# Streaming encoder step on one core: sums by pairs in three LayerNorms, high halves first, and a store for each output tile

## The reference, cut to what matters

```python
h = layernorm(x, ln_in_g, ln_in_b)
p = h @ w_in                                  # RWKV-7 columns, then q, k, v, f of FoX attention
mix = concat(rwkv7(p_r), fox(p_f)) @ w_out
h = layernorm(alpha * h + mix, ln1_g, ln1_b)
q = h @ peer_w_q                              # 8 heads; scores, top 16 of 16384 experts per head
act = gelu(peer_u[idx] . h)
h = layernorm(alpha * h + sum(gate * act * peer_v[idx]), ln2_g, ln2_b)
```

## Time and profile before

| | |
|---|---|
| median of 3 runs | 1433.5 us (1433.44 to 1434.15) |
| the profiled execution's own time | 1433.6 us |
| its span in the profile | 1431.9 us |
| PE busy | 1381.3 us, 96% of the span |
| DVE, ACT, POOL busy | 987.8, 685.0, 494.0 us |
| mean granted clock of PE | 0.994 of 2.4 GHz |

### The profile page before, as it was taken

One profiled execution on the slowest core, in us unless ns is written; L12 is line 12 of the kernel. 1 busy time (PEld: TensorE's weight loads), 2 busy tenths in 40 slices (PEclk: granted clock), 3 DMA queues, 4 the chain that ended last, 5 costly groups with the idle time before them and its releaser, 6 DMA issues.

```text
span 1431.9 us, 34642 instructions
## 1 busy us (share of the span) xinstructions
PE 1381.3 (96%) x11341; PEld 1320.5 (92%) x11341; DVE 987.8 (69%) x2303; ACT 685.0 (48%) x1455; POOL 494.0 (34%) x664
## 2 busy tenths in 40 slices
PE   7999999889999999999999999999999999999996
PEld 5977787778899999999999999999999999999995
DVE  5348776675699995888888888856555555555555
ACT  4665533223436666544444444444444544444444
POOL 4000021111538998766666666652000000000000
PEclk9999999999999999999999999999999999999999
DMA  4352110004324445444444444445555555555552
GB/s 137 125 144 81 60 46 3 3 10 163 102 76 118 140 139 144 136 124 118 120 122 117 120 122 118 123 133 147 148 152 147 148 151 147 149 152 147 148 152 81
DMA packets 85224, 168.69 MB, mean 118 GB/s; under 512 B 9850, under 2 KB 11402, under 8 KB 84970
## 3 DMA queue, kind: packets, MB, share of 16 engines
q1 hardware_dynamic: 85162, 167.84, 40.6%
HBM read 164.80 MB, written 2.97 MB: 117 GB/s over the span
## 4 chain that ended last, share of the span: by engine, by line
PE 55%; POOL 23%; issue 12%; DVE 6%; ACT 2%; POOLq 1%; DMA 0%; ACTq 0%; SPq 0%; DVEq 0%
POOL hlo L635 23%; PE PS L1040 15%; PE PS L1042 15%; PE PS L1041 15%; PE PS L1134 1%; PE PS L1035 1%; POOLq L633 1%; PE PS L1028 1%; DVE TT L1533 1%; PE PS L1299 1%; PE PS L1422 1%; DVE FSQ L1733 1%; DVE GSD L1696 1%; PE PS L1316 1%; PE PS L1314 0%
## 5 line engine op out<-in xcount | busy, mean ns | idle before, releaser
L635 POOL TENSOR_TENSOR hlo<-hraw,hhiq 128x256 fp32r<-128x256 f32 x512 | 397.2, 785 | 145.1 <-ACT hhiq L678 143.2
L1040 PE MATMUL PS<-H1h,hhiq 128*128 128x320 f32 x1024 | 343.6, 336 | 3.9 <-POOL hlo L635 3.4
L678 ACT ACTIVATE hhiq<-hraw 128x256 fp32r<-128x256 f32 x508 | 211.4, 418 | 257.1 <-PE PS L1042 228.4
L1042 PE MATMUL PS<-H1h,hlo 128*128 128x320 f32 x1024 | 315.4, 308 | 0.0
L1041 PE MATMUL PS<-H1l,hhiq 128*128 128x320 f32 x1024 | 315.1, 308 | 0.0
L1042 PE MATMUL PS<-Wh,hlo 128*128 128x320 f32 x1016 | 314.0, 309 | 0.0
L1040 PEld LDWEIGHTS PS<-H1h,hhiq 128*128 128x128 f32 x1024 | 193.6, 189 | 9.2 <-POOL hlo L635 7.0
L1041 PEld LDWEIGHTS PS<-H1l,hhiq 128*128 128x128 f32 x1024 | 193.4, 189 | 0.0
L1042 PEld LDWEIGHTS PS<-H1h,hlo 128*128 128x128 f32 x1024 | 192.2, 188 | 0.0
L1042 PEld LDWEIGHTS PS<-Wh,hlo 128*128 128x128 f32 x1016 | 190.7, 188 | 0.0
L1953 DVE TENSOR_SCALAR oh<-iotak,pair 128x128 f32<-128x128 f32 x320 | 128.6, 402 | 48.4 <-PE PS L1458 43.8
(11 more groups left out here) (324 smaller groups left out, 2543.9 us busy)
## 6 DMA issues: line engine op xcount, KB each, us to landing
hraw<-in_uT SPq DMA_DIRECT2D x256, 256.0 KB, 2.6
hraw<-in_vE SPq DMA_DIRECT2D x254, 256.0 KB, 2.6
wraw<-in_wbig SPq DMA_DIRECT2D x50, 512.0 KB, 3.8
xin<-in_xT SPq DMA_DIRECT2D x4, 336.0 KB, 4.3
out_yT<-XF SPq DMA_DIRECT2D x4, 320.0 KB
ckx<-in_ckT SPq DMA_DIRECT2D x2, 512.0 KB, 7.6
vs<-in_cv SPq DMA_DIRECT2D x1, 768.0 KB, 8.5
out_ko<-kx SPq DMA_DIRECT2D x1, 672.0 KB
```

Source lines behind the costliest of these rows:

```text
L635: nc.gpsimd.tensor_tensor(hlo[q // 2 % 4][:, cols_], hraw[q // 2 % 4][:, cols_], hhiq[q % 4][:].bitcast(F32), ALU.subtract).then_inc(s_hlo ...
L678: return nc.scalar.activation(out, in_, f, **kw)
L1040: mm(out, whi_, xhi, start=start, stop=False)
L1042: return mm(out, wlo_, xhi, start=False, stop=stop)
```

## The change

It has six parts.

1. **Sums by pairs.** In norm 0 DVE adds x in pairs as its parts land and PE sums two tiles instead of eight. In every norm the squares of tiles 4 and 5, and of 6 and 7, are added on DVE (`norm_pairs`) so that PE sums six tiles instead of eight. In norm 2 POOL adds tiles 0 to 3 of XF (XS4) and DVE tiles 6 and 7 (XS2), and PE sums four.
2. **Ones in front.** PE begins with `hold(7, 8)`.
3. **Order of the loads.** x goes before `colv`; the first weights before the small matrices, which get a semaphore of their own (`s_rest`). POOL makes the low half of item 0.
4. **High half first.** The V products and those of items 34 and 35 do the two matmuls with the high half of an activation tile when that is there, and the one with the low half after it. In w_q's case the high halves of the weights 35 and 36 are made ahead of the squares, and 37 behind them.
5. **The last sums.** DVE makes XF tile by tile as each bank is finished (`s_fin`). ACT loads the table for the root beforehand. DVE applies gain and bias to tiles 6 and 7.
6. **Stores.** One store for each of the 8 tiles.

```diff
-NORM_ORDER = [list(range(KT)), list(range(KT)), [2, 3, 0, 1, 4, 5, 6, 7]]
+PAIRS = ((0, 1, 2, 3, 4, 6), (0, 1, 2, 3, 4, 6), (0, 1, 2, 3, 4, 6))
-POOL_ITEMS = [*range(I_WQ, N_ITEMS)]
+POOL_ITEMS = [0, *range(I_WQ, N_ITEMS)]
...
+                if i == 0:
+                    sp.dma_start(wfs[:], wf).then_inc(s_small, 16)
...
-            for q in range(4):
-                sp.wait_ge(s_yf, 2 * q + 2)
-                sp.dma_start(yT[:, 2 * q:2 * q + 2, N_META:T], XF[:, 2 * q:2 * q + 2, :]).then_inc(s_out, 16)
+            for j in (0, 1, 2, 3, 4, 6, 5, 7):
+                if j < KT - 2:
+                    sp.wait_ge(s_yf, j + 1)
+                else:
+                    sp.wait_ge(s_yd, j - KT + 3)
+                sp.dma_start(yT[:, j, N_META:T], XF[:, j, :]).then_inc(s_out, 16)
...
+            for k in range(1, 4):
+                pool.wait_ge(s_xf, k + 1)
+                if k > 1:
+                    pool.wait_ge(s_xs4, k - 1)
+                nc.gpsimd.tensor_tensor(XS4[:], XF[:, 0, :] if k == 1 else XS4[:], XF[:, k, :], ALU.add).then_inc(s_xs4, 1)
...
-            for i in range(I_WO + 2, I_WQ + 1):
+            for i in range(I_WO + 2, I_WQ + 3):
                 whi_of(i)
             norm_squares(1, X1, SQ1)
-            whi_of(I_WQ + 1)
+            whi_of(I_WQ + 3)
...
             pe.wait_ge(s_onesg, 1)
-            for j in range(KT):
-                pe.wait_ge(s_x[j // (KT // XQ)], 16)
-                mean_part(0, j, xin, ones)
+            hold(7, 8)
+            for q in range(0, XQ, 2):
+                pe.wait_ge(s_xp, q // 2 + 1)
+                ins = mm(PS[:, MEAN_BANK, 0:T], ones[:], SQ0[:, q, :], start=(q == 0), stop=(q == XQ - 2))
+            ins.then_inc(s_mean, 1)
...
+            for q in range(XQ):
+                dve.wait_ge(s_x[q], 16)
+                pair = tt(SQ0[:, q, :], xin[:, 2 * q, :], xin[:, 2 * q + 1, :], ALU.add)
+                if q % 2:
+                    own(pair)
+                    tt(SQ0[:, q - 1, :], SQ0[:, q - 1, :], SQ0[:, q, :], ALU.add).then_inc(s_xp, 1)
+            norm_center(0, xin)
+            norm_pairs(0, SQ0)
...
+            def norm_pairs(n, S):
+                for k in (4, 6):
+                    dve.wait_ge(s_sq, KT * n + k + 2)
+                    tt(S[:, k, :], S[:, k, :], S[:, k + 1, :], ALU.add).then_inc(s_sqp, 1)
...
+            mean = PS[:, MEAN_BANK, 0:TQ]
+            for j in (4, 5):
                 pe.wait_ge(s_xf, j + 1)
-                mean_part(2, j, XF, ones2)
+                mm(mean, ones2[:], XF[:, j, :], start=(j == 4), stop=False)
+            pe.wait_ge(s_xs4, 3)
+            mm(mean, ones2[:], XS4[:], start=False, stop=False)
+            pe.wait_ge(s_xs2, 1)
+            mm(mean, ones2[:], XS2[:], start=False, stop=True).then_inc(s_mean, 1)
```

More of the change, by code:

```diff
@@ L273, in build @@
         SDF = last.put("SDF", [P, TQ])
+        XS4 = last.put("XS4", [P, TQ])
+        XS2 = last.put("XS2", [P, TQ])
         m = Region(BASE, TAIL)
@@ L680, in norm_squares @@
             def norm_squares(n, X, S):
-                for j, k in enumerate(NORM_ORDER[n]):
+                for j, k in enumerate(range(KT)):
                     act.wait_ge(s_xc, KT * n + j + 1)
@@ L1014, in _ @@
                     down(k * 2 + e, e, k * 16 + 16 * e)
+            act.wait_ge(s_onesg, 2)
+            act.wait_ge(s_down, NI)
+            own(A(SDF[:, 0:1], ones2[:, 0:1], ACT.Sqrt))
             norm_squares(2, XF, SQF)
             norm_root(2, SDF[:])
-            for j in range(KT):
+            for j in range(KT - 2):
                 act.wait_ge(s_nr, 2 * KT + j + 1)
@@ L1026, in mean_part @@
             def mean_part(n, j, X, c1):
-                ins = mm(PS[:, MEAN_BANK, 0:X.shape[2]], c1[:], X[:, NORM_ORDER[n][j], :], start=(j == 0), stop=(j == KT - 1))
+                ins = mm(PS[:, MEAN_BANK, 0:X.shape[2]], c1[:], X[:, j, :], start=(j == 0), stop=(j == KT - 1))
                 if j == KT - 1:
@@ L1032, in variance @@
             def variance(n, S, c1):
-                for j, k in enumerate(NORM_ORDER[n]):
-                    pe.wait_ge(s_sq, KT * n + j + 1)
-                    ins = mm(PS[:, VAR_BANK, 0:S.shape[2]], c1[:], S[:, k, :], start=(j == 0), stop=(j == KT - 1))
+                for k in PAIRS[n]:
+                    if k < 4 or len(PAIRS[n]) == KT:
+                        pe.wait_ge(s_sq, KT * n + k + 1)
+                    else:
+                        pe.wait_ge(s_sqp, 2 * sum(len(x) < KT for x in PAIRS[:n]) + k // 2 - 1)
+                    ins = mm(PS[:, VAR_BANK, 0:S.shape[2]], c1[:], S[:, k, :], start=(k == 0), stop=(k == PAIRS[n][-1]))
                 ins.then_inc(s_var, 1)
@@ L1153, in _ @@
                     k = 2 * i + kk
+                    w, v = whi[hi_slot(i)][:, 512 * kk:512 * kk + 512], wlo[raw_slot(i)][:, 512 * kk:512 * kk + 512]
+                    pe.wait_ge(s_hhi, k + 1)
+                    for b, t0 in enumerate(V0):
+                        mm(PS[:, 4 + b, :], hTh[:, k, t0:t0 + P], w, start=(k == 0), stop=False)
+                        mm(PS[:, 4 + b, :], hTh[:, k, t0:t0 + P], v, start=False, stop=False)
                     pe.wait_ge(s_hlo, k + 1)
                     for b, t0 in enumerate(V0):
[L1156 to L1158 removed]
+                        ins = mm(PS[:, 4 + b, :], hTl[:, k, t0:t0 + P], w, start=False, stop=(k == KT - 1))
                 ins.then_inc(s_item, 1)
@@ L1423, in scores_of_head @@
                 ins.then_inc(s_scp, 1)
+            split(I_WQ)
+            split(I_WQ + 1)
             for k in range(KT):
+                cols_ = slice(P * k, P * k + P)
+                pe.wait_ge(s_h1h, k + 1)
+                for i in (I_WQ, I_WQ + 1):
+                    mm(PS[:, i % 2, 0:TQ], whi[hi_slot(i)][:, cols_], H1h[:, k, :], start=(k == 0), stop=False)
+                    mm(PS[:, i % 2, 0:TQ], wlo[raw_slot(i)][:, cols_], H1h[:, k, :], start=False, stop=False)
                 pe.wait_ge(s_h1l, k + 1)
                 for i in (I_WQ, I_WQ + 1):
-                    item(i, H1h, H1l, ks=range(k, k + 1))
+                    ins = mm(PS[:, i % 2, 0:TQ], whi[hi_slot(i)][:, cols_], H1l[:, k, :], start=False, stop=(k == KT - 1))
+                    if k == KT - 1:
+                        ins.then_inc(s_item, 1)
             for i in range(I_WQ + 2, N_ITEMS):
@@ L2037, in _ @@
             dve.wait_ge(s_h1s, KT)
-            for j, k in enumerate(NORM_ORDER[2]):
-                if j % NJ == 0:
-                    dve.wait_ge(s_down, 2 * NI - 1 + j // NJ)
+            for k in range(KT):
+                dve.wait_ge(s_fin, k + 1)
                 v.scalar_tensor_tensor(XF[:, k, :], H1s[:, k, :], ALPHA, PS[:, k, 0:TQ], ALU.mult, ALU.add).then_inc(s_xf, 1)
             dve.wait_ge(s_xf, KT)
+            tt(XS2[:], XF[:, KT - 2, :], XF[:, KT - 1, :], ALU.add).then_inc(s_xs2, 1)
             norm_center(2, XF)
+            norm_pairs(2, SQF)
             norm_root(2, XF, SDF[:])
@@ L2046, in _ @@
                 tt(XF[:, j, :], XF[:, j, :], SDF[:], ALU.mult).then_inc(s_nr, 1)
+            for j in range(KT - 2, KT):
+                dve.wait_ge(s_nr, 2 * KT + j + 1)
+                v.tensor_scalar(XF[:, j, :], XF[:, j, :], col("ln2_g", j), col("ln2_b", j), ALU.mult, ALU.add).then_inc(s_yd, 1)
 def kernel(**inputs):
```

48 lines of the change are left out of this document (22 added, 26 removed).

## The result

| | before | changed kernel |
|---|---|---|
| median, us | 1433.47 (8 runs, 1431.01 to 1434.58) | 1426.85 (8 runs, 1424.74 to 1429.05) |
| ratio, 95% interval | | 0.9955 [0.9944, 0.9966] |
| profiled execution | 1433.6, span 1431.9 | 1425.49, span 1423.8 |

The change takes 6.6 us off, 0.45%. The forecast was 1424.9 with a range of 1422.9 to 1428.2. So the sum has to be gone through stage by stage.

A forecast was written before the change was run, and what follows sets the result against it. PE, busy 96% of the span, was taken as the bound, with gains left only where it waits: front 2.8, middle 2.7 and tail 3.2 sum to 8.7 us off 1433.6, giving 1424.9, range 1422.9 to 1428.2.

The forecast's parts named there:

- rival B: PE's idle pieces lower its clock (front 1.1 us, tail up to 1.7), or POOL is late; about 1427.2, chance 0.24.
- Front, 2.8: Start through norm 0: earlier center and shorter variance make the first hTh tile end 2.8 us earlier.
- what clock?: Norm 0's mean: PE's last matmul, two steps, taken at 1.2 GHz, 1.13 us; center at 9.7, 2.1 us gained.
- 0.7 gained: Norm 0's variance: ends 5.2 us after the center's start instead of 5.92, if PE is at 2.4 GHz again.
- V order, 0: V products, high half first: could start 0.7 us earlier, but item 1 waits for DVE's low half; 0 gained.
- Item 0's low half on POOL: Front: moved from DVE, it takes 2.4 us, starts some 14.3, ends by 17, ahead of PE's need at 18.9.
- Middle, 2.7: Norm 1 and w_q: variance 0.65 us gained and item 36's earlier start 2.05, together 2.7.
- The w_q term: w_q: after the last H1l only its two matmuls are left; item 36 starts at 368.6 instead of 370.64, 2.05 us gained.
- Tail, 3.2: After the last down matmul: center 2.1 us, variance 0.5, scaling to last store 0.2, smaller last store 0.4; 3.2 gained.
- Clock of the tail: Norm 2's variance at half clock costs up to 1.7 us; part of rival B, whose whole chance is 0.24.
- Rival C: Gain given back: another half-clock chunk-stage stretch (1.7 us) or POOL in `up` (2); about 1426.8 to 1427.6, chance 0.08.
- Rival D: Slower: a late load holds ACT ahead of norm 1's squares and stops the chain; over 1436.4, chance 0.02.

The follow-up runs named there:

- e5: Changed kernel with 14 instead of 8 ones matmuls in front, 6 between the two matmuls of norm 0's mean and 4 behind; 1424.54 us, ratio 0.994.
- e6: Changed kernel with PE summing all eight tiles of x for norm 0's mean, behind the ones in front, without DVE's pairs of x; 1425.55 us, ratio 0.9956.
- e9: e6 with five more ones matmuls in the wait between norm 0's mean and variance; 1426.1 us, ratio 0.9955.
- e10: e9 with six ones matmuls per 128-token group but the first, in PE's wait for DVE in the chunk stage; 1421.8 us, ratio 0.9925.
- e4: Changed kernel with the front put back as before (norm 0, load order, V products, item 0's low half); 1427.63 us, ratio 0.9956.
- e8: Changed kernel with V products waiting for each activation tile's low half again, as before; 1426.25 us, ratio 0.9959.
- e11: Changed kernel with the weights' early high halves back where the kernel before had them, w_q's new product order kept; 1430.37 us, ratio 0.9982.

## Why the prediction came right, and where it didn't

The forecast's total came out right because two of its three stretches did, and because the range had room for rival B, which took the third. By its own steps:

- **Front, 2.8: wrong.** The step that failed is "what clock?", and what was built on it: "0.7 gained" in the variance "if PE is at 2.4 GHz again". It took 1.2 GHz for the last matmul of the mean alone and expected the clock up for the variance. PE stayed at, or fell back to, 1.2 GHz for nearly all of it, with steps 0.56 apart, which the prediction itself had named as a sign of being wrong: center to root took 7.85 in the first trace instead of 5.2, and 5.39 where the gaps were filled (e5, e6, e9, e10). The front brought nothing, by e4's ratio and by the mean over traces, and 1.9 with the gaps filled. This is rival B's first half, at a cost of 1.8 on average (7.2 for 5.39, and 1.2 to 2.5 from trace to trace) and not 1.1. The other 0.9 of the 2.8 is mostly the starting point: the trace of before had its center at 11.78, where the mean of four traces is 11.19. In the changed kernel's trace the center itself was 0.56 late (10.26 for 9.7): x's last part landed at 7.63 instead of 7.1, and its steps were at 1.2 GHz, as said.
- **V order, 0: right** (e8), for the reason given.
- **Item 0's low half on POOL: hidden, as said,** but it started at 15.90 instead of 14.3 and ended at 18.25 instead of 17. POOL's own list of selects came first, which the prediction left out: in e6 it ran to 15.0, and in the changed kernel 0.8 longer, since selects take longer beside DVE's adds (the third pair 0.95, and 0.69 in e6, which has no such adds).
- **Middle, 2.7: right in its mechanism, 2.2 in size** in all traces that have it whole. The variance gave 0.47, not 0.65: from the last pair's end (352.83 + 1.11 = 353.94) to the root it took 0.89 for the 0.7 assumed. The w_q term was 1.7, not 2.05: when the last H1l was there (365.50), PE still had matmuls of the last tile's high half to do, and it took up the last two low ones at 365.82 instead of at once. e11 shows that it hangs on the early halves alone, and that without them the clock can be lost besides.
- **Tail, 3.2: right, 3.18.** Center 2.08 for 2.1, variance 0.47 for 0.5, scaling to the end 0.65 for 0.6. XS4's chain took 2.90 for 2.85, and the center came 2.33 behind the end of the last down matmul for 2.35.
- **Clock of the tail (rival B's second half): didn't occur;** the variance's first eight steps took 2.42 there.
- **Rival C:** stretches at half clock do move between executions (one to three in the chunk stage of the traces here), and the changed kernel's first trace had, as far as can be told, the better draw: 2.2 us in a stage without an edit. e10 shows that they are a loss that can be had back.
- **Rival D: out.** ACT waited for DVE's X ahead of the squares of norm 1, never for a load.

Sum: 0 + 2.2 + 3.2 = 5.4, against 6.6 in the medians; by the ratio's interval the change takes off 4.9 to 8.0 us, so the two agree, and the 1.2 between them isn't accounted for. The profiled execution's 8.1 comes near the forecast's 8.7 by chance: -0.5 in the front, and 3.2 from the two stretches without an edit, whose length differs between executions (`up` and `down` took 980.2 to 982.6 us over the fourteen traces).

## What to carry to other kernels

A shorter chain for PE need not be the faster one: here fewer matmuls, each behind another engine's add, left PE idle between short pieces, the clock stayed at its lower level, and the work behind paid back all that the shorter sum had gained. Count the gaps as well as the steps, and try harmless matmuls in them, on a bank that is free, ahead of the wait. Compare variants at a point behind which all of them run alike: the first product started earlier here without anything behind it being earlier. Where the times of a kernel spread by a few microseconds, look for stretches at half clock behind PE's waits; filling PE's waits ahead of them brought 4.3 us here, more than any part of the change. In a tail in which nothing else runs, sums moved to idle engines and a finer grain of stores came out as counted.
